# Decode's dense slots of a hybrid MoBA and mLSTM step: values next to the next slot's scores, both halves of the gate pieces ahead of the third key turn, and seven pieces moved there from the last slots

## What is computed

```
def _moba_sample(q, k, v, cache_k, cache_v, page_table):
    ...
    if nb_full > 0:
        kb_past = cache_k[page_table[:, :nb_full * ppb]].reshape(DB, nb_full, MOBA_BLOCK, H, D)
        k_mean = jnp.mean(kb_past, axis=2, dtype=jnp.float32)
        idx, valid = _moba_select(q, k_mean, nb_full)
        ...
    return _moba_core(q, k_sel, v_sel, valid, k_own, v_own, own_mask)

def _merge_mlp(x, att, ml, ga, gm, ...):
    ya = att.reshape(B, S, A_W) @ w_attn_br
    ym = ml.reshape(B, S, M_W) @ w_mlstm_br
    u = jax.nn.sigmoid(ga) * ya + jax.nn.sigmoid(gm) * ym
    ...
```

## Time and profile before

| | us |
|---|---|
| median of 3 runs | 1071.86 |
| lowest, highest | 1069.09, 1075.05 |
| profiled execution, its own time | 1072.29 |
| its span from first to last instruction | 1070.7 |
| TensorE busy (matmuls) | 1045.9 |
| VectorE, ScalarE, GpSimd busy | 627.4, 482.7, 203.2 |
| bytes moved | 153.16 MB |

### The profile page before, as it was taken

How to read it: one execution, slowest core, us unless ns; L and a number is a source line. 1 busy time by engine, 2 the same in 40 slices (tenths; PEclk the granted TensorE clock), 3 DMA queues, 4 the chain that set the end, 5 groups by cost and what they waited for, 6 DMA issues and landing times.

```text
span 1070.7 us, 20807 instructions
## 1 busy us (share of the span) xinstructions
PE 1045.9 (98%) x7518; PEld 892.3 (83%) x7518; DVE 627.4 (59%) x1240; ACT 482.7 (45%) x1029; POOL 203.2 (19%) x280
## 2 busy tenths in 40 slices
PE   8999999999999999999999999999999999999997
PEld 7987878887878877777779988998899889889985
DVE  5254435544775666555553857448787358347756
ACT  5362233323554465555552446345256136424641
POOL 4004011221001023333332010100341034024200
PEclk9999999999999999999999999999999999999999
DMA  6522215224125889999976271122432432343322
GB/s 208 159 73 57 69 50 149 60 79 138 41 64 154 257 285 342 322 344 331 331 233 202 75 245 40 57 83 69 118 99 82 126 89 82 116 118 89 109 89 88
DMA packets 114417, 153.16 MB, mean 143 GB/s; under 512 B 9598, under 2 KB 66435, under 8 KB 114323
## 3 DMA queue, kind: packets, MB, share of 16 engines
q1 hardware_dynamic: 99808, 106.98, 32.1%
q0 software_dynamic: 13120, 44.08, 12.3%
q10 hardware_dynamic: 1394, 0.83, 0.3%
HBM read 144.76 MB, written 7.10 MB: 142 GB/s over the span
## 4 chain that ended last, share of the span: by engine, by line
PE 81%; DVE 7%; DMA 5%; issue 2%; SPq 2%; ACT 2%; POOLq 0%; POOL 0%; ACTq 0%
PE ps L479 27%; PE ps L2708 13%; PE ps L929 7%; PE ps L516 6%; PE ps L487 4%; PE ps L945 4%; PE ps L452 4%; DMA kring<-in_cache_k_dram 4%; PE ps L1963 4%; PE ps L2004 2%; PE ps L1972 1%; SPq L1928 1%; PE ps L1093 1%; PE ps L1113 1%; SPq L1930 1%
## 5 line engine op out<-in xcount | busy, mean ns | idle before, releaser
L361 DVE TENSOR_TENSOR w<-w,w 128x512 fp32r<-128x512 f32 (+1 forms) x192 | 137.2, 724 | 161.0 <-ACT w L350 155.9
L350 ACT ACTIVATE w<-w 128x512 fp32r<-128x512 f32 (+1 forms) x192 | 115.0, 608 | 191.9 <-PE ps L487 131.9
L479 PE MATMUL ps<-w,hid 128*128 128x512 f32 x672 | 161.6, 389 | 0.0
L479 PEld LDWEIGHTS ps<-w,hid 128*128 128x128 f32 x672 | 125.9, 188 | 26.2 <-issue 0.2
L479 PE MATMUL ps<-w,hT 128*128 128x512 f32 x576 | 145.0, 401 | 0.0
L929 PE MATMUL ps<-hT,w 128*128 128x288 f32 x768 | 126.8, 307 | 0.0
L479 PEld LDWEIGHTS ps<-w,hT 128*128 128x128 f32 x576 | 106.0, 190 | 24.7 <-issue 3.2
L929 PEld LDWEIGHTS ps<-hT,w 128*128 128x128 f32 x768 | 105.1, 188 | 12.3 <-issue 11.6
L1930 POOL DMA_DIRECT2D vring<-in_cache_v_dram x128 | 68.9, 538 | 171.6 <-issue 171.6
L2134 DVE COPY kT<-ps 128x512 f32<-128x512 f32 x64 | 44.1, 689 | 74.9 <-PE ps L1963 74.5
L1963 PEld LDWEIGHTS ps<-ident,kring 128*128 128x128 f32 x512 | 56.6, 140 | 36.2 <-DMA kring<-in_cache_k_dram 27.0
(11 more groups left out here) (403 smaller groups left out, 1789.0 us busy)
## 6 DMA issues: line engine op xcount, KB each, us to landing
kring<-in_cache_k_dram SPq DMA_DIRECT2D x128, 256.0 KB, 4.2
vring<-in_cache_v_dram POOLq DMA_DIRECT2D x128, 256.0 KB, 4.5
w<-in_w_in_dram SPq DMA_DIRECT2D x88, 256.0 KB, 2.8
w<-in_w_down_dram SPq DMA_DIRECT2D x64, 256.0 KB, 2.7
w<-in_w_up_dram SPq DMA_DIRECT2D x40, 256.0 KB, 2.9
b<-in_w_up_dram SPq DMA_DIRECT2D x36, 256.0 KB, 4.0
w<-in_w_out_dram SPq DMA_DIRECT2D x16, 256.0 KB, 2.9
x<-in_x_prompt_dram SPq DMA_DIRECT2D x4, 512.0 KB, 6.8
```

Source lines behind the costliest of these rows:

```text
L350: eng.activation(spread(w_hi, n, j, width), together(w32, n, j, width), ACT.Copy)\
L361: eng.tensor_tensor(spread(w_lo, n, j, width), together(w32, n, j, width), spread(w_hi, n, j, width).bitcast(F32), ALU.subtract).then_inc( ...
L479: mm = eng.matmul(ps[:, t, :], left[a][:, k, prompt_cols(t)], w[b][:, j, :], start=(k == 0 and (a, b) == THREE[0]), stop=(k == kt - 1 and ...
```

## The change

The dense slots with s % 4 = 3 (7, 11, ..., 31) get two pieces instead of one, and the last slots give up seven. In all dense slots every half piece stands ahead of the third key turn and none behind the values, so that values are followed by the next slot's scores. The last slots keep their halves on both sides of the values.

```
--- before.py
+++ after.py
@@ -979,8 +979,8 @@
         if s < VALS:
             return 2
         if s < ALL_GROUPS:
-            return 1
-        return (3, 2, 2, 3, 2, 2, 2, 0)[s - ALL_GROUPS]
+            return 2 if s % GROUPS == 3 else 1
+        return (2, 1, 1, 2, 1, 1, 1, 0)[s - ALL_GROUPS]
 
     def pieces_at(g):
         return 2 - g % 2 if g < A_SLOTS else pieces_in(g - A_SLOTS)
@@ -2035,14 +2035,15 @@
                     own_turn((s - VALS) // GROUPS)
             if s % GROUPS == 3 and s >= GROUPS + VALS + 1:
                 out_turn((s - GROUPS - VALS - 1) // GROUPS)
-            for _ in range(pieces_in(s)):
+            together = VALS <= s < ALL_GROUPS
+            for _ in range((2 if together else 1) * pieces_in(s)):
                 next(main)
             if s < ALL_GROUPS:
                 keys_turn(s, 2)
                 keys_turn(s, 3)
             if VALS <= s < ALL_GROUPS + VALS:
                 values(s - VALS)
-            for _ in range(pieces_in(s)):
+            for _ in range(0 if together else pieces_in(s)):
                 next(main)
 
     def out_cols(dst, b, g):
```

## The result

| | before | with the change |
|---|---|---|
| median, us | 1072.18 (4 runs) | 1087.41 (4 runs) |
| lowest, highest | 1069.09, 1075.05 | 1084.04, 1092.23 |
| ratio of the two, 95% interval | | 1.014 [1.0113, 1.0167] |
| profiled execution, its own time | 1072.29 | 1084.04 |
| its span | 1070.7 | 1082.5 |

The change makes the kernel slower by 1.4%. The direction was forecast. The time, 1081, is 6.4 us too low, and the measured median lies 0.4 us above the range. The profiled execution is the fastest of the four; it is 2.6 us above the 1081.4 forecast for it.

A forecast was written before the change was run, and what follows sets the result against it. The prediction took the two-group key ring to bound the dense slots: +12.3 us until slot 32's scores, -3.2 in the last slots, sum +9.1 on the profiled 1072.29, so 1081.4, stated as 1081 us; range 1071 to 1087.

The forecast's parts named there:

- (1): Dense slots: values next to scores save TensorE 7.5 us over 26 slots, but the key ring is held longer.
- R: Residence: a dense slot's first key turns to the end of its last; 3.3 us before, forecast 4.10, or 5.75 with two pieces.
- (2): Slots 7, 11, ..., 31: a second piece adds 1.65 us before the third turn; four more weight loads; vector work costs nothing.
- (3): Sum for the dense slots: twelve odd-ring hops take 171.9 us, +11.1 (ends +5.1 and +17.1); slot 31 adds 1.4.
- L: Time from freeing half the key ring until the next keys have landed there; forecast 9.4 us, between 8.9 and 9.9.
- (4): Border of values and scores: waiting for VectorE's copy of head 3's keys costs 0 us, at most 0.1 to 0.2 a slot.
- (5): Last slots: 11.7 us of matmuls leave, but GpSimd's value pages set the pace, so only 3.2 us is saved.
- A(7): Start of slot 7's first two key turns, forecast about 0.2 us earlier; A(31) is the same point in slot 31.
- weight loads decide: Rival, slower than forecast: key pages queued with weight loads land late, L reaches 9.9, +15 us, 1087; no separate chance given.
- What would show it: Profile signs: key wait over 35 us, no ScalarE wait, dense slots about 172, idle times before L929 gone, last slots about 36.
- The rule on tiling modes: Changing tiling mode drains TensorE; by this rule alone, fewer changes in dense slots make the kernel 7.5 us faster.
- The ring: Key buffer of two groups in dense slots: every second slot follows no faster than R plus L.

The follow-up runs named there:

- the filled waits: Changed kernel plus 46 and 38 unused identity transposes ahead of the values of slots 34 and 37: 1085.28 us, 1.0102 of the kernel before.
- the change once more: The changed kernel unedited, three executions on the chip of the quarter-load run: 1092.78 us, 1.0181 of the kernel before.
- the split order: Kernel before, old table; in dense slots one half ahead of the third key turn, the other between last turn and values: 1070.55 us, 0.998.
- the one-half order with the new table: Changed kernel with only one half ahead of the third turn in dense slots, the rest between last turn and values: 1077.97 us, 1.0062 of before.
- spread loads: Old table, half the halves behind the last key turn, second weight load of each pair one slot later: 1071.25 us, 0.998 of before.
- the written-out form: Changed kernel with GpSimd's hardware loop over the sequences written out: 1088.2 us, 1.0159 of the kernel before.
- the quarter loads: Changed kernel with weight loads of slots 7 to 30 cut to a quarter of the bytes: 1079.6 us, 1.0082 of the kernel before.
- order-only: Kernel before with the change's order of halves but the old table of pieces: 1076.09 us, 1.0031 of the kernel before.

## Why the prediction was right in direction and wrong in size

- **(1) The order.** Right in mechanism, each side of it. The drains: forecast 7.5 us of work over 26 slots at 0.3, so 7.2 for these 24; measured 5.5 us of TensorE's busy time, 0.23 a slot, inside the bounds of 0.2 to 0.4 but near the lower. R: forecast 4.10 in a slot with one piece; 4.1 measured, and 4.4 where own scores stand inside.
- **(2) The pieces.** R of 5.75 forecast, 5.58 measured in slot 7. Their vector work was costed at nothing under cover of the key waits. In the change it is so (0.4 us of ScalarE wait); in the kernels whose key waits had shrunk ScalarE's copy came out at 4 to 5 us. It is hidden under the cover that was named, and shows without it.
- **(3) The dense slots.** 171.9 forecast, 171.1 in the profiled execution; L of the odd half 9.4 forecast, 9.23 measured; slot 31 +1.4, measured +1.3. The term holds for that execution. What it lacked is a spread: an execution with L of 9.64 took 179.1, where 59.1 + 12 x 9.64 gives 174.8. The difference is the clock, which made the twelve R add up to 62.7 us.
- **(4) The border.** 0 forecast, 0 measured.
- **(5) The last slots: the step that failed.** -3.2 us forecast, +1.7 measured, 4.9 too low. The term put at nothing was TensorE's clock. I had read the clock of before, 1.00 in both windows, and written that it "plays no part", while the same part forecast that TensorE would stand without work for several microseconds at a time. By the rows after, in order: group 28 comes 0.5 us later than forecast (the page behind the stall goes out 10.84 us behind the scores of slot 32, before 10.36). The values of slot 34 and the pieces behind them run at the lower clock. It reaches the value pages by the ring: the waits at the first pages of groups 30 and 31 are 1.67 and 1.57 us, with the filled waits 0.89 and 0.80, together +1.6. The last page lands in 5.5 instead of 4.3 us, +1.2, which is not the clock's. So the last values start at 35.75 us, forecast 32.5. From there to the output's turn 600.41 - 595.08 = 5.33 us pass in the second spell, where 36.2 - 32.5 = 3.7 were forecast, +1.6. Sum: 0.5 + 1.6 + 1.2 + 1.6 = 4.9, of which some 3.1 are the clock's. With the clock held and a landing of 4.3 us, the filled waits give 36.8 us against the forecast 36.2. The size is that of one execution; the change once more had 39.3 us, and the kernels that differ from it in weight loads alone 37.6 and 38.1, each over the 36.2.
- **What the miss is made of.** These 4.9 us, less 0.8 in the dense slots, less 1.3 since A(7) came 1.5 earlier and not 0.2, and less 0.1 in slot 31, are the 2.6 us (by rounding 2.7) by which the profiled execution is over the forecast. Of the 6.4 us by which the median is over 1081, 3.4 more are the distance from that execution, the fastest, to the median, and 0.4 the step from 1081.4 to 1081. The 3.4 us fit the spread under (3); no execution at the median was traced.
- **The range** ended at 1087 with L = 9.9. The median came there by another way, as far as two profiled executions tell: L was 9.23 and 9.64, and the lower clock, in the last slots of both and in the dense slots of one, made up the rest. The chance of 0.66 for slower was on the right side; the rival "weight loads decide" names the measured time, by L = 9.9, which neither execution had. That weight bytes cost some 10 us in whole runs speaks for part of it. Whether turn-taking between queues is how they do it, no run here shows.
- **What would show it.** A(7) to A(31) about 172: yes. L929's idle times gone, ScalarE's wait nearly gone (0.4 us), value-page waits in the last slots: yes. PEld's key wait over 35: 31.2 came. The last slots at 36: 41.1 came.
- **The rule on tiling modes** gave a gain of 7.5 us on TensorE by itself. The Trainium skill (TensorEngine Tiling (Array Packing), Key Properties) says that a change of tiling mode drains TensorE. The trace agrees: the order of the change and the split order both halve the number of such changes in a slot, and both save 5.5 us of busy time. The ring decides what of it is seen: +0.3% for the change's order, -0.2% for the split one.

The two halves of the change cost 3.3 us (0.31%) and 6.6 us (0.62%) alone and 15 to 19 together. The rest, 5 us or more, comes where both meet. Four halves ahead of the third turn (R of 5.6 to 5.7) are what the change has and neither of its halves has. Key waits of over 3 us on the weight-load side, with spells of lower clock in some executions, go with it, but the split order and the one-half order with the new table show one each, too. How the 5 us divide among them is not measured. The version to keep is the split order with the old table, at 0.998 of the time before in two sets of runs (the second with spread loads); no experiment had a clear gain from moving pieces out of the last slots.

## What to carry to other kernels

Where transfers bound a ring, work placed between the first and the last use of its buffer is paid in the ring's period, even if it removes drains: put it behind the release. Before emptying a stage of "useless" filler work, find what it waits for once it is empty, and price the clock that may fall in the gaps: here an idle time of a few microseconds mostly cost more than itself. Where a kernel is near such gaps, ask for the spread between executions too, and not for the profiled one alone.

## What the hardware showed that was not expected

- TensorE's granted clock was at its lower level (0.50, 1.2 GHz) for 3.4 or 6.8 us at idle times of 5.16, 4.78, 4.34, 3.11, 3.08, 2.93, 2.80 and 2.27 us, among others. The spell began between 2.0 us ahead of the idle time's end and 1.8 us behind it. Waits of 2.58 us in the change's own profile, 2.51 and 2.57 with the filled waits, 2.87 in the written-out form and 2.92 with the quarter loads left it at 1.00. The length of one idle time alone doesn't say what follows.
- Idle time is not the only thing that a spell follows. In seven of the fourteen profiles, that of the kernel before among them, one of 3.4 us (in one 6.8) stands at 129 to 131 us, in a stretch in which TensorE is busy all the time (10.00 of the 10 us from 120 to 130).
- GpSimd's issue of a value page stalls once, by 3.3 to 3.4 us, between the first and the second page of group 28: in all fourteen profiles, in the loop and written out, whatever the time. The longer idle times at the first page of a group are waits for the ring.
- The same program's dense slots took 171.1 and 179.1 us in two profiled executions. The order-only and the split-order kernels, whose longest key waits are 2.4 and 1.9 us on the weight-load side against 3.5 and 3.8, spread over 5.6 and 4.5 us in nine whole runs each; the change spread over 8.2 us in its first four.
